# Attention in groups of 512 queries, with V as the stationary operand, in a hybrid decoder layer

## The reference

```
L = 16 + 2048;  scale = 1 / sqrt(192)
for each head:
    s = (q @ k.T) * scale            # q, k: (L, 192)
    s[i, j] = -inf where j > i
    p = softmax(s, axis=-1)
    o = p @ v                        # v: (L, 128)
o_mla[:, head] = o                   # norm and output projection follow in a later stage
```

## Time and profile before

| | us |
|---|---|
| median of 3 runs | 3686.16 (3685.36 to 3688.68) |
| the profiled execution | 3679.25 |
| its span, of which PE busy | 3677.8, 3235.0 (88%) |
| DVE, ACT, POOL busy | 1603.7, 1219.9, 580.3 |
| stretch from the first load of the attention stage to its last PE work | 1279 to 1820 |
| mean granted PE clock, share of 2.4 GHz | 0.935 |

### The profile page before, as it was taken

The page is one execution under the profiler, slowest core; times in us unless marked ns, Lnnn a source line. Parts: engine busy times, 40 slices in busy tenths (PEclk is TensorE's granted clock), DMA queues, the critical chain, the costliest instruction groups (busy, mean ns, idle before and its releaser), DMA issues. The chain is left out here.

```text
span 3677.8 us, 55042 instructions
## 1 busy us (share of the span) xinstructions
PE 3235.0 (88%) x20547; PEld 2695.5 (73%) x20547; DVE 1603.7 (44%) x2494; ACT 1219.9 (33%) x2323; POOL 580.3 (16%) x971
## 2 busy tenths in 40 slices
PE   7995749993999789999759959999999999999998
PEld 6884548993777657766547748887888788878887
DVE  2114633432444366566477624432454245424542
ACT  3213522222344344445333324422332133213321
POOL 1112420003656300000045410000000000000000
PEclk9997879996899889999879979999999999999999
DMA  5443454222343240120046542244433433343322
GB/s 164 144 131 98 120 187 155 78 73 62 80 88 82 66 125 28 57 65 29 20 156 210 171 144 80 80 137 132 112 99 126 133 109 100 125 133 108 102 80 103
DMA packets 408414, 394.58 MB, mean 107 GB/s; under 512 B 42458, under 2 KB 333734, under 8 KB 405302
## 3 DMA queue, kind: packets, MB, share of 16 engines
q1 hardware_dynamic: 369286, 286.21, 26.8%
q0 software_dynamic: 26240, 91.67, 7.9%
q10 hardware_dynamic: 12720, 14.42, 1.2%
HBM read 284.92 MB, written 107.30 MB: 107 GB/s over the span
## 5 line engine op out<-in xcount | busy, mean ns | idle before, releaser
L2224 DVE TENSOR_TENSOR ff_w_lo<-ff_w_raw,ff_w_hi 128x2048 fp32r<-128x2048 f32 (+1 forms) x176 | 309.2, 1759 | 573.0 <-ACT ff_w_hi L2189 573.0
L2189 ACT ACTIVATE ff_w_hi<-ff_w_raw 128x2048 fp32r<-128x2048 f32 (+1 forms) x176 | 261.8, 1488 | 495.2 <-PE ff_pD L2304 346.3
L2282 PE MATMUL ff_pG<-ff_u_hi,ff_w_hi 128*128 128x512 f32 x704 | 278.4, 395 | 34.5 <-DVE ff_w_lo L2224 34.5
L2304 PE MATMUL ff_pD<-ff_w_hi,ff_g_hi 128*128 128x512 f32 x704 | 274.6, 390 | 4.5 <-DVE ff_yb L2254 3.5
L2282 PE MATMUL ff_pG<-ff_u_lo,ff_w_hi 128*128 128x512 f32 x704 | 277.5, 394 | 0.0
L2282 PE MATMUL ff_pG<-ff_u_hi,ff_w_lo 128*128 128x512 f32 x704 | 277.3, 394 | 0.0
L2282 PE MATMUL ff_pU<-ff_u_hi,ff_w_hi 128*128 128x512 f32 x704 | 276.4, 393 | 0.0
L2282 PE MATMUL ff_pU<-ff_u_hi,ff_w_lo 128*128 128x512 f32 x704 | 274.3, 390 | 0.0
L2282 PE MATMUL ff_pU<-ff_u_lo,ff_w_hi 128*128 128x512 f32 x704 | 274.0, 389 | 0.0
L2304 PE MATMUL ff_pD<-ff_w_lo,ff_g_hi 128*128 128x512 f32 x704 | 274.0, 389 | 0.0
L2304 PE MATMUL ff_pD<-ff_w_hi,ff_g_lo 128*128 128x512 f32 x704 | 273.9, 389 | 0.0
(11 more groups left out here) (346 smaller groups left out, 6893.8 us busy)
## 6 DMA issues: line engine op xcount, KB each, us to landing
ff_w_raw<-in_w_gate SPq DMA_DIRECT2D x88, 512.0 KB, 4.0
ff_w_raw<-in_w_up SPq DMA_DIRECT2D x88, 512.0 KB, 5.2
ff_w_raw<-in_w_down SPq DMA_DIRECT2D x176, 256.0 KB, 2.9
scr_tok<-pj_tok POOLq DMA_DIRECT2D x17, 548.0 KB, 3.1
scr_uT<-pj_u_hi POOLq DMA_DIRECT2D x17, 512.0 KB, 4.6
scr_uT<-pj_u_lo POOLq DMA_DIRECT2D x17, 512.0 KB, 6.6
scr_yT<-cv_y SPq DMA_DIRECT2D x8, 1088.0 KB, 4.0
scr_dtok<-cv_ob SPq DMA_DIRECT2D x8, 1088.0 KB, 5.7
```

What stands on the lines that cost most here:

```text
L2189: act.activation(w_hi[s][:, 0:w], w_raw[s][:, 0:w], ACT.Copy).then_inc(w_half[s], 1)
L2224: dve.tensor_tensor(w_lo[s][:, 0:w], w_raw[s][:, 0:w], f(w_hi[s][:, 0:w]), ALU.subtract).then_inc(w_ready[s], 1)
L2282: m = pe.matmul(bank[s][:, :], a[s][:, o:o + P], x[:, k, :], start=(k == 0 and n_pass == 0), stop=(k == KD - 1 and n_pass == 2))
L2304: m = pe.matmul(pD[t][:, :], x[:, ft, t * P:t * P + P], a[s][:, i * 512:i * 512 + 512], start=(ft == 0 and n_pass == 0), stop=(ft == FT - ...
```

## The change

The attention stage is rewritten.

- Queries come in 16 groups (`ORDER`: four heads by four groups of 512 queries, `GW`), without a padding tile; the loop over turns is gone and the program is written out. The 16 meta tokens as queries are computed apart at the start, for all heads (`sm`, `om`).
- The key grid is moved: key step 0 of a group is the 16 meta keys, and each further step 128 keys (`STEPS` = 5, 9, 13 or 17 for a group). Scores of a query tile are cut in pieces of 128n columns with 16 more in the first (`cut`), at most 512 wide, 5, 9, 13 and 17 pieces a group, into four banks `pS`.
- In `values` V is stationary and the group's transposed probabilities move: V hi by `pt_hi`, V lo by `pt_hi`, V hi by `pt_lo`, 512 columns each, fewer in the last three steps of a group. The output `pO` is transposed; ACT copies it to `oT`, PE transposes it in four tiles, DVE multiplies with the inverse sum (`norm`), and one DMA stores 512 rows.
- `turn` transposes one key step of the four query tiles. Transposes run one step ahead and use two banks (`TURN`), probabilities three buffers (`NPX`). The scores of group n+1 are spread over the steps of group n (`issued`) and end two steps before its end; the exponentials of a tile follow in the step after its last piece (`finished`), in place in `rows`.
- K, the rotary part and V are loaded straight into the buffers of the lo half, in four parts (`SPLITS`), and split part by part (`SPLIT_AT`), for the next head during groups 1 to 3.
- `v` in DRAM is stored with one row for each position.

```diff
-                act.dma_start(S["v"][:, :, bass.ds(t, 1), :].rearrange("h p j d -> p (h j) d"), kv[s][:, :, NOPE:]).then_inc(v_stored[s], 16)
+                act.dma_start(S["v"][:, bass.ds(t * P, P), :].rearrange("h p d -> p h d"), kv[s][:, :, NOPE:]).then_inc(v_stored[s], 16)
...
+        ORDER = [(h, g) for h in range(HEADS) for g in range(GROUPS)]
+        STEPS = [QB * (g + 1) + 1 for _, g in ORDER]
+        NPS, NPT, NPX = 4, 2, 3
...
+        def issued(n, m):
+
+            if n + 1 == NG:
+                return []
+            count, room = len(PIECES[ORDER[n + 1][1]]), STEPS[n] - 2
+            return [k for k in range(count) if k * room // count == m]
...
+        def turns(n, m):
+
+            out = []
+            if m + 1 < STEPS[n]:
+                out = ([(n - 1, None)] if m == 1 and n else []) + [(n, m + 1)]
+            if m == STEPS[n] - 1 and n + 1 < NG:
+                out.append((n + 1, 0))
+            return out
...
+            def load_q(n):
+                h, g = ORDER[n]
+                s = n % 2
+                cols = slice(N_META + GW * g, N_META + GW * (g + 1))
+                if n >= 2:
+                    sp.wait_ge(qk_done, PB[n - 1])
+                sp.dma_start(f(q_lo[s][:, :]), S["qT"][h, 0:NOPE, cols]).then_inc(q_loaded[s], 16)
...
+            sp.wait_ge(id_made, 2)
+            load_q(0)
+            load_head(0, 0, 2)
+            for n, name in enumerate(("qT", "kT")):
+                sp.dma_start(qkm[:, n, :, :], S[name][:, 0:NOPE, 0:N_META].rearrange("h d t -> d h t")).then_inc(m_loaded, 16)
+                sp.dma_start(qkm_rope[:, n, :, :], S[name][:, NOPE:QK, 0:N_META].rearrange("h d t -> d h t")).then_inc(m_loaded, 16)
+            sp.dma_start(vm_raw[:, :, :], S["v"][:, 0:N_META, :].rearrange("h p d -> p h d")).then_inc(m_loaded, 16)
+            load_head(0, 2, EARLY)
+            load_q(1)
+            load_head(0, EARLY, NS)
...
+            def exp(n, i):
+                g = ORDER[n][1]
+                w = N_META + P * (QB * g + i + 1)
+                act.wait_ge(maxed, QB * n + i + 1)
...
+            for n in range(NG):
+                for m in range(STEPS[n]):
+                    if m == 0 and n:
+                        outputs(n - 1)
+                    for tn, tm in turns(n, m):
+                        if tm is not None:
+                            hi(tn, tm)
+                    if m:
+                        for i in finished(n, m - 1):
+                            exp(n + 1, i)
+                    if m == 1 and n + 2 < NG:
+                        split_q(n + 2)
+                    for h, x in SPLIT_AT.get((n, m), []):
+                        split(h, x)
...
+            def turn(n, m):
+                x = TURN[n, m]
...
+                    if m == 0:
+                        pe.wait_ge(p_ready, QB * (n + 1))
+                    for i in range(first_tile(m - QB * ORDER[n][1]), QB):
+                        row = rows[n % 2][i]
+                        if m == 0:
+                            t = pe.transpose(pT[x % NPT][0:N_META, i, :], row[:, 0:N_META], ident[:, :])
+                        else:
+                            at = N_META + P * (m - 1)
+                            t = pe.transpose(pT[x % NPT][:, i, :], row[:, at:at + P], ident[:, :])
...
+                for y, (a, p) in enumerate(((v_hi, pt_hi), (v_lo, pt_hi), (v_hi, pt_lo))):
+                    t = pe.matmul(pO[n % 2][:, at:GW], a, p[x % NPX][part, at:GW], start=(m == 0 and y == 0),
+                                  stop=(m == STEPS[n] - 1 and y == 2), skip_group_check=True)
                 t.then_inc(pv_done, 1)
...
+            for n in range(NG):
+                for m in range(STEPS[n]):
+                    for tn, tm in turns(n, m):
+                        turn(tn, tm)
+                    for k in issued(n, m):
+                        scores(n + 1, k)
+                    values(n, m)
```

More of the change, by code:

```diff
@@ L1448, in stage_attention @@
         r = Room(nc, ctx, "at")
[L1449 to L1459, removed]
@@ L1469, in stage_attention @@
[L1469 to L1476, removed]
@@ new lines, in stage_attention, with cut @@
+        NPS, NPT, NPX = 4, 2, 3
+        WIDEST = [max(N_META + P * (QB * g + i + 1) for _, g in ORDER[x::2] for i in range(QB)) for x in range(2)]
+        def cut(i):
+            nb = i + 1
+            n = -(-(P * nb + N_META) // 512)
+            base, extra = divmod(nb, n)
+            at, out = 0, []
+            for k in range(n):
+                end = at + P * (base + (k >= n - extra)) + (N_META if k == 0 else 0)
+                out.append((i % QB, k, at, end, k == n - 1))
+                at = end
+            return out
@@ L1481, in stage_attention @@
+        o_sb = [r.sb(f"o_sb{i}", [P, QB, VD]) for i in range(2)]
         ident = r.sb("ident", [P, P])
@@ new lines, in _ @@
+            pe.wait_ge(m_loaded, 80)
+            for h in range(HEADS):
+                cols = slice(h * N_META, h * N_META + N_META)
+                pe.matmul(pO[0][0:N_META, cols], qkm[:, 0, h, :], qkm[:, 1, h, :], start=True, stop=False)
+                t = pe.matmul(pO[0][0:N_META, cols], qkm_rope[:, 0, h, :], qkm_rope[:, 1, h, :], start=False, stop=True)
+            t.then_inc(meta_pe, 1)
+            for k in range(len(PIECES[0])):
+                scores(0, k)
+            pe.wait_ge(meta_dve, 6)
@@ new lines, in _ @@
+            for h in range(HEADS):
+                t = pe.transpose(pO[1][0:N_META, h * N_META:h * N_META + N_META], sm[3][:, h, :], ident[0:N_META, 0:N_META])
+            t.then_inc(meta_pe, 1)
+            pe.wait_ge(meta_act, 2)
+            for h in range(HEADS):
+                t = pe.matmul(pO[0][0:N_META, h * VD:h * VD + VD], sm_turned[:, h, :], vm_raw[:, h, :], start=True, stop=True)
+            t.then_inc(meta_pe, 1)
+            turn(0, 0)
+            for n in range(NG):
+                for m in range(STEPS[n]):
+                    for tn, tm in turns(n, m):
+                        turn(tn, tm)
+                    for k in issued(n, m):
+                        scores(n + 1, k)
+                    values(n, m)
@@ L1780, in stage_out @@
+            turn(NG - 1, None)
 def stage_out(nc, A, S):
```

543 lines of the change are left out of this document (293 added, 250 removed).

## The result

| | before | after |
|---|---|---|
| median, same chip | 3687.42 us (3685.36 to 3692.20) | 3639.50 us (3638.67 to 3648.99) |
| ratio | | 0.9874, interval 0.9855 to 0.9893 |
| profiled execution | 3679.25 | 3648.99 |

The change takes 48 us off (1.3%); 16 were forecast. The profiled execution of before lies 8 us under its median and that of after 9.5 over its own, so these two traces differ by 30 only.

What follows compares the result with a forecast made beforehand. PE was taken to bound the attention stage: work 405, waits 55, unexplained 13, clock 31, start and end 2 - 2 gave 504 us for 520, so 3686 - 16 = 3670 us. The range was 3635 to 3702.

Steps and rivals of the forecast that it cites:

- work with the unexplained part: Attention stage: PE's work falls from 445 to 405 us; 15 us unexplained before, 13 of them carried over.
- waits: Attention stage: PE's waits on other engines, 34 us before, become 26 + 24 + 5 = 55.
- clock: Attention stage: loss to the lower clock, 26 us before, becomes 31: 27 at twelve group changes, 4 at the start.
- start, end: Stage's edges: 2 us gained at the start, 2 lost at the end by a longer tail and larger store.
- PE's work: Attention stage: scores 223 us, values 108, transposes 69, meta key steps 5; sum 405, 40 less than before.
- (a): Group changes: PE waits for the next group's exponentials, 1.8, 2.2 and 2.7 us, 26 in all.
- (b): Fourth group: 53 steps at the pace of their chain lose 15 us, splits and exponentials 9 more; 24 in all.
- (c): Third group: steps with one score piece and one exponential of up to 2 us wait 5 us in all.
- The 9 us for copies that push between: Fourth group: next head's splits and exponentials get between copy and subtraction, 3 us in each of three heads.
- The work shows in full: Faster rival: waits between groups stand, fourth group at chain pace, clock falls at half the changes; 3635 us, chance 0.25.
- The clock pays for the waits: Slower rival: a long clock fall follows each of twelve group changes, 4.5 to 6.7 us lost each; 3700 us, chance 0.15.
- The clock falls in the fourth group: Slower rival: PE's 0.28 us idle in each of 53 steps brings the lower clock; 3713 us, chance 0.05.

Runs made afterwards that it cites:

- two second profiles: The kernel before and the changed kernel each run once more, nothing edited, for another profile: 3678.71 us before, 3640.01 us changed.
- whole: Changed kernel with the K, rope and V parts of one group split one behind the other in one step instead of four: 3642.62 us, ratio 0.9886.
- noahead: Changed kernel with each step's transposes directly ahead of its values instead of one step ahead: 3789.43 us, ratio 1.0285.
- fill: Changed kernel with 6, 8 or 11 useless matmuls ahead of the first transposes at the twelve group changes: 3618.02 us, ratio 0.9834.
- twoahead: Changed kernel with transposes two steps ahead, three banks each for transposes and scores, next group's scores issued three steps sooner: 3599.83 us, ratio 0.9777.
- earlier: Changed kernel with transposes two steps ahead, three banks each, next group's scores four steps sooner: 3620.58 us, ratio 0.9838.
- ps3: Changed kernel with three score banks instead of four, nothing else: 3630.32 us, ratio 0.9872.
- twoahead_late: Changed kernel with transposes two steps ahead, three banks each, next group's scores only one step sooner: 3612.72 us, ratio 0.9806.
- The fourth product: Changed kernel with a fourth values matmul in each step, V lo by probabilities lo: 3652.53 us, ratio 0.9917.

## Why the prediction was half right

Its direction and most of its mechanism hold; the size is off by a factor of three, for the most part by one term, the waits. Before against after, from the two second profiles, term by term of its sum:

| term | predicted | measured |
|---|---|---|
| work with the unexplained part | 460 to 418: -42 | 457 to 414: -43 |
| waits | 34 to 55: +21 | 33.0 to 30.5: -2.5 |
| clock | 26 to 31: +5 | 26.5 to 31.7 (first profile 38.6): +5 |
| start, end | -2, +2 | 0, -3.8 |
| stage | -16 | -44 |

**PE's work** is right as a sum by errors that cancel. A full step costs 0.80 and not 0.69, as the first values matmul holds the next one for 0.34 behind a score piece or a wait, and for 0.31 to 0.32 behind transposes; but there are 28 of them a head and not 32 (the counts of the new profile, below), and four transposes take 0.35, not 0.41. Full steps so come to 112 x 0.80 = 90 us against the 88 taken, transposes to 672 x 0.35 / 4 = 59 against 69. By the remainder, tails, first steps and small gaps took some 10 more than allowed; they were not taken apart.

```profile
L1894 PE MATMUL at_pO<-at_pt_lo,at_v x160: 273/394/629, 1327.0 to 1789.5; 128*128 128x512 f32 x112, 128*128 128x384 f32 x16, 128*128 128x256 f32 x16, 128*128 128x128 f32 x16
...
L1871 PE MATMUL at_pT<-at_ident,at_row x544: 269/272/474, 1308.6 to 1788.3; 128*128 128x128 f32 x182
```

**(a), the waits between groups**: predicted 1.8, 2.2 and 2.7, 26 in all, measured 1.71, 2.14 and 2.70 from start to start, 22.9 in all as idle time. Their clock, predicted 27: 29.0 in the first profile, 20.5 in the second. That the whole clock term meets its 31 in the second profile is luck: the changes lost 6.5 less, and the start lost 11.2 and not 4.

**(b), the fourth group, is the step that failed**: 24 us of waits for the subtraction predicted, at most 7.3 measured together with (c). The pace was right (1.38 foretold, 1.415 measured). Wrong was to charge it to 53 steps, and the splits on top. With transposes one step ahead the chain limits a pair of steps, (0.80 + 2.07)/2, so a score piece of 1.0 us covers its neighbours too: three steps with one piece are 3 x 1.15 + 1.0 = 4.45 of work against 3 x 1.415 = 4.25 of chain. The waits left in the fourth groups of the first three heads, 4 or 5 in each, sum to 1.3 to 2.2 a group. The full loss stands in the last group alone, 13 full steps of 0.26 from start to start, 3.4, of which the profile shows 2.1 as idle. The 9 us for copies that push between are refuted by whole: even clumped they cost 2.3 of wait.

**(c), the third group**: 5 predicted; PE has no wait inside any third group.

**Start and end**: the first score at 10 and the first transposes at 23.5 were foretold (11 and 22). Not foretold is that the clock then stays down for 19 to 22 us more instead of 5, 10 to 11 us of the term clock where 4 were allowed. The end gained 3.8 instead of losing 2: the stage closes 6.4 us behind PE's last instruction, with the larger store, where it took 10.2. Why was not tried.

**The rivals.** "The work shows in full" had the outcome almost to the microsecond (3635, measured 3640), with waits of 41 and a clock of 18; measured are 31 and 32 to 39. The two misses cancel, so its outcome is luck, though it was nearer than the forecast on the fourth group (15 for 24). "The clock pays for the waits" needed 3.6 us lost at each change from which it decides; measured are 2.4 and 1.7 as means of twelve. "The clock falls in the fourth group" did not happen, and noahead shows at what gap it does.

**Blind in the prediction**: that the large copies of before cost 31 us. The prediction has them "take nothing from PE by themselves; the waits that they caused are in the 34"; true, and the clock behind these waits was in the 26. The 11 us at the turn of the loop stood in the same two terms. The changed kernel is free of both and spends 43 to 52 us at its twelve changes instead (22.9 idle, 20.5 or 29.0 of clock). That is why 43 us less work end as 44 in the stage and not as more, and what fill and twoahead take back in part.

## What to carry to other kernels

Count a chain's loss over a pair or a row of steps, not step by step: with a lead of one step, any work on PE in the neighbourhood pays for it. Waits of nearly the same sum cost very differently, by the length of the single wait: twelve at changes, the longest 2.4 us idle, lost 20 to 29 us to the clock; twelve of 1.5 to 2.1 lost 5; 48 of 0.6 on average lost 5. But 94 of 1.1 on average, close behind each other, lost over 100. So shorten or spread the longest first, and look at their distance; where one can't be shortened, filling it can pay, as 100 useless matmuls took 14 us off this stage. An instruction for work far ahead can also come too early: in earlier it kept back the engine's own next transposes. When a rewrite changes work and schedule at once, try the cheap part of it alone in the old kernel: cutting and spreading the big copies gave 31 of its 48 us.

## What the hardware showed unexpectedly

- In four profiles with the same idle times at the changes (two of after, ps3, whole) the granted clock fell at 3 of 16 of 1.43 us, at 9 of 16 of 1.87, and at all 16 of 2.42, for 3.4 to 10.2 us at a time. In twoahead and twoahead_late it fell at 4 of 11 of 2.1. So the same kernel had nine such falls in one execution and six in another, and M differed by 7 us; the kernel before had the same seven twice.
- The gates and delta stages, ahead of attention and the same in all kernels, took together from 401.6 to 414.3 us in these profiles, as the clock cost it 50.6 to 65.5. Differences of under 10 us between two kernels are only told by a stage's own account.
- The fourth product, 39 us more of work, cost 20 us of the stage (12.5 by the medians): fuller waits, and a clock that fell less often.
- At the upper clock a values matmul of 512 columns with its own weight load starts 0.23 behind the one before it; the second of a step starts 0.31 to 0.34 behind the first.
